# Two transformer blocks on one NeuronCore: one plain fp32 matmul in place of three rounded fp32 ones, and four weight slots filled in one order

## What is computed

```python
def first_block(x, c, ctx, ...):
    sh1, sc1, g1, sh2, sc2, g2 = adaln(c, w_ada)          # six vectors of 1024
    hc = modulate(rms_norm(ctx), ...)                     # 256 context tokens
    s_f, s_b = hgrn2_context_states(hc @ w_in ...)        # start states of the scans
    hx = modulate(rms_norm(x, norm_mix), sh1, sc1)
    mx = token_mix(hx)       # hx @ w_in (1024 x 4096), gated scans in two directions,
                             # a 3-tap convolution, then @ w_out (1024 x 1024)
    x = x + g1 * mx
    x = x + g2 * expert_choice_ffn(...)   # 16 experts, 64 tokens each, width 2048
    return rms_norm(x, norm_final)

def second_block(x, p, ...):
    z = rmsnorm(x, g_mix) @ w_in_2        # 1024 x 4376
    h = x + (ga * attention(z) @ w_o + gb * conv31(z) @ w_conv_out) @ w_out_2
    v = causal_dwconv(rmsnorm(h, g_ffn) @ w_up_2)         # 1024 x 5632
    h = h + (gelu(v_gate) * v_val) @ w_down_2             # 2816 x 1024
    h = h + sigmoid(rmsnorm(h, g_ple) @ w_ple_gate) * (p @ w_ple)
    return rmsnorm(h, g_final)
```

## Time and profile before

| | |
|---|---|
| Median of three runs | 2591.15 us |
| The profiled execution's own time | 2587.63 us |
| Its span, first to last instruction | 2585.7 us |
| Mean granted TensorE clock | 0.931 |
| TensorE busy with matmuls (PE) / weight loads (PEld) | 2221.8 us (86%) / 1390.3 us (54%) |
| VectorE / ScalarE / GpSimd busy | 900.8 / 564.9 / 368.1 us |
| Split of the weights: ScalarE L354, VectorE L360, GpSimd L367 | 163.0 / 211.6 / 235.8 us |
| Moved by DMA | 529.07 MB |

### The profile page before, as it was taken

One profiled execution on the slowest core, in us unless ns is written; L12 is line 12 of the kernel. 1 busy time (PEld: TensorE's weight loads), 2 busy tenths in 40 slices (PEclk: granted clock), 3 DMA queues, 4 the chain that ended last, 5 costly groups with the idle time before them and its releaser, 6 DMA issues.

```text
span 2585.7 us, 23858 instructions
## 1 busy us (share of the span) xinstructions
PE 2221.8 (86%) x10085; PEld 1390.3 (54%) x10085; DVE 900.8 (35%) x1266; ACT 564.9 (22%) x872; POOL 368.1 (14%) x261
## 2 busy tenths in 40 slices
PE   5999988778887878787878777899889989999987
PEld 3887766433232324232323222478557867887865
DVE  3435545400100101010101010477785537665443
ACT  3442303200000000000000000431545324333443
POOL 4111201000000000000000000130432413223530
PEclk8999989789899999998989898998889999999999
DMA  7121415379999999999999999134001223332220
GB/s 252 55 72 38 164 36 205 118 279 369 340 376 360 379 367 358 372 374 350 371 356 366 371 344 371 69 83 131 1 33 65 98 73 98 98 98 90 90 82 33
DMA packets 248017, 529.07 MB, mean 205 GB/s; under 512 B 13091, under 2 KB 41481, under 8 KB 247912
## 3 DMA queue, kind: packets, MB, share of 16 engines
q1 hardware_dynamic: 247336, 527.09, 56.4%
q0 software_dynamic: 576, 0.46, 0.1%
HBM read 525.43 MB, written 2.10 MB: 204 GB/s over the span
## 4 chain that ended last, share of the span: by engine, by line
PE 62%; DMA 19%; DVE 8%; ACT 5%; issue 4%; POOL 1%; SPq 0%; ACTq 0%; DVEq 0%
PE bank L849 12%; PE bank L511 10%; PE bank L512 10%; PE bank L513 10%; DMA f<-in_w_up_dram 9%; PE bank L889 8%; DMA f<-in_w_gate_dram 8%; PE bank L522 2%; PE bank L757 2%; DVE r L360 1%; DMA f<-in_w_down_dram 1%; PE bank L823 1%; PE bank L714 1%; PE bank L724 1%; PE bank L560 1%
## 5 line engine op out<-in xcount | busy, mean ns | idle before, releaser
L849 PE MATMUL bank<-f,high 128*64 128x512 f32 x2048 | 499.3, 644 | 124.3 <-DMA f<-in_w_gate_dram 65.6
L367 POOL TENSOR_TENSOR r<-f,r 128x1024 fp32r<-128x1024 f32 (+3 forms) x86 | 235.8, 2762 | 1819.0 <-ACT r L354 1818.9
L511 PE MATMUL bank<-r 128*128 128x512 f32 (+1 forms) x952 | 381.1, 400 | 39.3 <-DVE r L1984 12.9
L849 PEld LDWEIGHTS bank<-f,high 128*64 128x64 f32 x2048 | 173.1, 148 | 432.1 <-issue 422.2
L513 PE MATMUL bank<-r 128*128 128x512 f32 (+1 forms) x1016 | 401.4, 395 | 0.0
L512 PE MATMUL bank<-r 128*128 128x512 f32 (+1 forms) x952 | 377.1, 396 | 0.0
L889 PE MATMUL bank<-f,high 128*64 128x512 f32 x1024 | 259.6, 665 | 91.3 <-issue 80.5
L360 DVE TENSOR_TENSOR r<-f,r 128x1024 fp32r<-128x1024 f32 (+3 forms) x86 | 211.6, 2497 | 101.5 <-ACT r L354 101.5
L1928 DVE SCALAR_TENSOR_TENSOR f<-bank,low,f 128x512 f32<-128x512 f32 x64 | 48.1, 751 | 520.4 <-PE bank L837 516.8
L511 PEld LDWEIGHTS bank<-r 128*128 128x128 f32 (+1 forms) x952 | 181.3, 190 | 87.6 <-issue 33.8
L889 PEld LDWEIGHTS bank<-f,high 128*64 128x64 f32 x1024 | 90.7, 153 | 255.0 <-issue 255.0
(11 more groups left out here) (311 smaller groups left out, 2074.4 us busy)
## 6 DMA issues: line engine op xcount, KB each, us to landing
f<-in_w_down_dram SPq DMA_DIRECT2D x68, 2048.0 KB, 10.7
f<-in_w_gate_dram SPq DMA_DIRECT2D x64, 2048.0 KB, 12.6
f<-in_w_up_dram SPq DMA_DIRECT2D x64, 2048.0 KB, 12.5
f<-in_w_in_dram SPq DMA_DIRECT2D x15, 2048.0 KB, 7.8
f<-in_w_ada_dram SPq DMA_DIRECT2D x12, 2048.0 KB, 9.5
f<-in_w_up_dram SPq DMA_DIRECT2D x22, 1024.0 KB, 7.0
f<-in_w_out_dram SPq DMA_DIRECT2D x4, 2048.0 KB, 8.3
high<-in_x_dram SPq DMA_DIRECT2D x4, 1024.0 KB, 6.1
```

Of the source, the lines that this page charges most:

```text
L367: up(g.tensor_tensor(low_part(c)[:, z], whole(c)[:, z], high_part(c)[:, z].bitcast(F32), ALU.subtract), "lo_g", c, i)
L511: pe.matmul(o, wh, xh, start=first, stop=False)
L849: ins = pe.matmul(o[64 * e:64 * e + 64, :], xsT[p % 2][:, k, 64 * e:64 * e + 64], ws[e][:, k, :], start=k == 0, stop=k == 7)
```

## The change

Every product of `three` becomes one plain fp32 matmul of the undivided tiles. The split of weights and tokens goes, with its instructions on ScalarE, VectorE and GpSimd. All chunks of the kernel, the first two modulation slices and the experts' included, form one list; chunk c lies in slot c % 4, and a load waits for the last use of chunk c - 4. The normed tokens are written once (U1, U2) and kept; the second norm after attention goes. x is no longer loaded a second time: its raw transpose into XT is made at the start (32 more transposes there, 4 more copies on ScalarE and 4 on VectorE), and the 32 transposes and 8 copies before the output projection go. SBUF regions of the second block move.

```diff
-            def three(o, wh, wl, xh, xl, first, last):
-                pe.matmul(o, wh, xh, start=first, stop=False)
-                pe.matmul(o, wl, xh, start=False, stop=False)
-                return pe.matmul(o, wh, xl, start=False, stop=last)
...
+            def tiles(c, nk, n=512):
+                if c not in ready:
+                    ready.add(c)
+                    pe.wait_ge(s[f"w{c % 4}"], landed[c])
+                return whole(c)[:, 0:nk * n].rearrange("p (k n) -> p k n", k=nk)
...
-            def project(o, c, j, xh, xl, nk=8, m=128):
-                wh, wl = tiles(c, nk)
-                z = slice(128 * j, 128 * j + m)
+            def project(o, w, c0, x_, nk=8, m=128):
                 for k in range(nk):
-                    weights(c, k, nk)
-                    ins = three(o, wh[:, k, z], wl[:, k, z], xh[:, k, :], xl[:, k, :], k == 0, k == nk - 1)
+                    ins = pe.matmul(o, w[:, k, c0:c0 + m], x_[:, k, :], start=k == 0, stop=k == nk - 1)
                 return ins
...
         def whole(c):
-            return own(SLOT, slot_at[2 * pair[c]])
+            return own(SLOT, slot_at[c % 4])
...
+            load_chunk(0)
+            load_chunk(1)
+            for c in (2, 3):
                 for dst, src in cols(I["w_ada"][0], 512 * c, 512)(early[c]):
                     sp.dma_start(dst, src).then_inc(s[f"ada{c}"], 16)
...
+            load_chunk(VI)
+            for c in range(4, len(chunks)):
+                last_use = chunks[c - 4][1]
+                sp.wait_ge(s[last_use[0]], val(*last_use))
                 load_chunk(c)
...
+                pe.wait_ge(s[f"x{t // 2}"], 16)
+                for half in range(2):
+                    o = take(("xw", t, half), "v_pre" if half else "a_pre", "xw", t, half)
+                    up(turn_blocks(o, [xtok[:, t, 512 * half + 128 * j:512 * half + 128 * j + 128] for j in range(4)]),
+                       "pe_pre", "xw", t, half)
...
-            for t in range(4):
-                pe.wait_ge(s[f"x{t // 2}"], 32)
-                for half in range(2):
-                    o = take(("xr", t, half), "a_mix", "xr", t, half)
...
             def normed(gen, d, gain, r_):
-                if d > 1:
-                    name = "u2l_g" if d % 2 else "u2l_v"
-                    v.wait_ge(s[name], val(name, gen, d - 2))
-                f = FTS[gen][d % 2]
...
+                up(v.scalar_tensor_tensor(out=U2[:, d, :], in0=XT[:, d, :], scalar=gain[:, d:d + 1], in1=r_, op0=ALU.mult,
+                                          op1=ALU.mult), "u2", gen, d)
```

More of the change, by code:

```diff
@@ L76, in build_program @@
         cursor = [0]
-        rounded, full = {}, {}
+        full = {}
         def mem(n, at_=None):
@@ L133, in build_program @@
         stage = v3(mem(5 * 128, M + 11264), 5)
[L134 to L137, removed]
+        adatmp = [mem(512, M + 26624 + 512 * i) for i in range(2)]
+        U1 = v3(own(4096, M + 14336), 8)
         CF = v3(own(2048, M + 12288), 8)
@@ L342, in low_part @@
-        def low_part(c):
-            return memR(SLOT, slot_at[2 * pair[c]])[:, 0:chunks[c][1]]
-        def quarter(c, i):
-            step = chunks[c][1] // 4
-            return slice(step * i, step * i + step)
-        def a_divide(a, c, pieces=range(4)):
-            for i in pieces:
-                if i == 0:
-                    a.wait_ge(s[f"w{pair[c]}"], landed[c])
-                z = quarter(c, i)
-                up(a.activation(high_part(c)[:, z], whole(c)[:, z], ACT.Copy), "hi", c, i)
@@ new lines, in chunk, with ada_chunk @@
+        def chunk(parts, *last_use):
+            chunks.append((parts, last_use))
+            return len(chunks) - 1
+        def ada_chunk(c):
+            return chunk(cols(I["w_ada"][0], 512 * c, 512), "pe_ada", c)
+        ada_at = {c: ada_chunk(c) for c in range(2)}
+        ZF = chunk(cols(win, 512, 512), "pe_proj", "cgate", 0, 1)
+        VI = chunk(cols(win, 1536, 512), "pe_proj", "vctx", 1)
+        ZB = chunk(cols(win, 1024, 512), "pe_proj", "sigb", 3)
+        QC = chunk(cols(win, 0, 512), "pe_proj", "q", 3)
@@ new lines, in build_program @@
+        for p in range(8):
+            for fc in range(4):
+                for kind in range(2):
+                    for e in range(2):
+                        w = I["w_up" if kind else "w_gate"][0, 2 * p + e]
+                        moe_at[p, "up", kind, fc, e] = chunk(cols(w, 512 * fc, 512), "pe_up", p, kind, fc)
+            for kc in range(4):
+                for e in range(2):
+                    moe_at[p, "down", kc, e] = chunk(rows(I["w_down"][0, 2 * p + e], 512 * kc, 4), "pe_down", p, kc)
@@ L661, in conv_half @@
                 o = banks[bank_of["cv", which, j]]
-                wh, wl = tiles(c, 8)
-                z = slice(128 * j, 128 * j + 128)
+                w = tiles(c, 8)
                 for k in range(4 * part, 4 * part + 4):
-                    weights(c, k, 8)
-                    ins = three(o[:, :], wh[:, k, z], wl[:, k, z], UH[:, k, :], UL[:, k, :], k == 0, k == 7)
+                    ins = pe.matmul(o[:, :], w[:, k, 128 * j:128 * j + 128], U1[:, k, :], start=k == 0, stop=k == 7)
                 if part:
@@ L879, in tensor @@
                 for kc in range(4):
-                    n = 24 * p + 16 + 2 * kc
-                    ws = []
-                    for e in range(2):
-                        pe.wait_ge(s[f"m{(n + e) % 4}"], 16 * ((n + e) // 4 + 1))
-                        ws.append(v3(own(SLOT, slot_at[(n + e) % 4]), 4))
+                    ws = [tiles(moe_at[p, "down", kc, e], 4, D) for e in range(2)]
                     pe.wait_ge(s["hT"], val("hT", p, 3))
```

685 lines of the change are left out of this document (152 added, 533 removed).

## The result

The change makes the kernel slower: 2741.62 us (median of 4 runs, 2739.34 to 2744.05) against 2590.37 (4 runs, 2586.69 to 2592.34), a ratio of 1.0586 with a 95% interval of 1.0567 to 1.0604. The prediction was 2767 us with a range of 2738 to 2805: the side and the price of a product are right, the time is 25 us too long, and part of the relief came by another way than I had said. The profiled execution took 2744.05 us, its span is 2742.3.

A forecast was written before the change was run, and what follows sets the result against it. TensorE was taken to bound everything outside the experts, DMA the experts. The profiled 2587.6 us + 246 for dearer products - 70 for stalls gave 2764; with the median 3.5 us above the profiled run, 2767 us, range 2738 to 2805.

The forecast's parts named there:

- The price of a product: TensorE outside the experts: 0.858 us plain against 0.680 for three rounded matmuls, +246 us in all, bounds +235 to +287.
- Rival 2: Plain fp32 products cost 0.887 us each, as read from the experts: +40 us, 2807 us; chance 9%.
- rival 1: Passes of plain fp32 overlap, a product costs under 0.731 us and the kernel gets faster; chance 3%.
- rival 3: TensorE's clock falls under long fp32 work, a twentieth of it running low: +60 us, 2827 us; chance 3%.
- Rival 4: One order of slots lets the expert stage run at 379 GB/s, 1062 us, so 2725 us in all; chance 5%.
- Rival 5: Shortened chains are held by something else, so only -35 us of stalls go: 2802 us; chance 7%.
- The relief: TensorE stalls outside the experts that go with the split, plus small gaps among a product's three matmuls: -70 us.
- The start: -0.5: Before the first product: about 4 us of split wait go, 3.5 us of added transposes and copies stay: -0.5 us.
- Between the scans: Gap from forward scan's end through gates and convolution tiles: 39.8 us becomes about 33; with hidden product cost, -13 us.
- Output projection: After the last scan work: copies no longer behind a split, x's transposes gone; 9.6 us plus 2.9 overcharged, -12 us.
- The scores before the first scan: TensorE's 5.82 us wait behind VectorE's split and gates shrinks, a late copy remaining: -5 us.
- The waits at the merge, at the down projection and in attention: TensorE waits of 5.74, 3.19 and 3.23 us tied to splits or rounding: -8, -6 and -5 us.

The follow-up runs named there:

- Experiment 2: Changed kernel with three rounded matmuls of one constant tile per product, split still gone: 2504.1 us, ratio 0.9679 to the kernel before.
- experiment 5: Changed kernel with each fp32 product cut into two matmuls of 64 stationary columns, side by side: 2744.03 us against 2741.62.
- experiment 3: Changed kernel with loads outside the experts waiting for the chunk two before, not four: 2740.03 us against 2741.62.
- Experiments 1: Kernel before with splits and their waits kept, one plain fp32 matmul replacing the three rounded ones: 2792.34 us, ratio 1.0797.
- experiment 4: Changed kernel without its 32 extra transposes at the start: 2739.18 us; kernel before with 32 such transposes added: 2581.52 us, ratio 0.9978.

## Why the prediction was right, and where it was off

- **The price of a product: right.** Predicted 0.858 us, measured 0.859; the FFN's up stage (352 products) took 303.9 us where I had said 302. Experiment 2 against the changed kernel shows 243.6 us for the exchange alone, predicted 246; the medians give 237.5.
- **Rival 2 (0.887, as in the experts): wrong**, by the products' pace, by experiment 5 in the tiled form, and by the experts' own loads: 0.887 was a misreading of the earlier trace rows, and so was the upper bound of the price, 287 us, that rested on it; the 0.443 in rival 1 likewise is 0.429. Rival 1 (overlap, below 0.731) and rival 3 (the clock falls under long fp32 work) did not come: the clock in the FFN was 0.99 to 1.00.
- **Rival 4 (experts gain) and the four slots: nothing.** 1100 us as before, and experiment 3. Rival 5 (stalls stay) did not come either.
- **The relief: the term that was mis-sized.** Predicted 70, measured 88 in the profiles. The step that failed is "The start: -0.5"; it was -10.0. I had 4 us for the split and measured 7.7: I counted one split, and the chain had ScalarE's rounding, VectorE's share of the weights and the first tile's split in a row. And I charged 3.5 us for the transposes "at the low clock", while they kept the clock up and brought 2.3.
- **The other stalls, one by one.** Between the scans: 31.2 us remain where I had said 33, so -14.3 with the hidden products, predicted -13. Output projection: 25.7 us from the scans' end to its second part became 17.1, so -11.5, predicted -12. The scores before the first scan: 5.82 + 0.17 became 0.27 + 1.67, -4, predicted -5. The waits at the merge, at the down projection and in attention (5.74, 3.19 and 3.23) are gone, as predicted; of the norm chains one lost 5.25 us altogether, another only 1.4 (5.08 to 3.69). With the start these are most of what makes 131 us of idle time 74. The 6 us of small gaps between the three, which I called a guess, were some 10 (experiment 2).
- **Part of the relief is clock.** Outside the experts the clock rose from 0.93 to 0.96 ahead of them and from 0.96 to 0.98 behind; 0.03 of 490 us and 0.02 of 1000 us are about 35 us, an estimate that the rounding of the clock to 0.01 leaves open by some 10. With 57 us less idle time that makes 92 against the 88, so the two explain the relief within this error, and no finer split can be read from them.
- **What I had attributed wrongly.** I took all the relief for the removed split. Experiments 1 and 2 show that about 39 of the 88 us come with the plain product alone, some 30 of them because slower products hide splits without removing them. That does not change the forecast's sum, but it is another mechanism than the one I gave.
- **A term that I had not seen.** The second scan took 8 us longer than in other runs of the same code, because its modulation slices ran at the low clock (below). Without it the profiled execution would have been 8 us shorter, and the relief 96 instead of 88.

## What to carry to other kernels

Before pricing a leaner scheme, find the engine that sets the end and price only what the change does to it: here 835 us of work vanished from three other engines and bought at most 84 us, while 0.18 us more for each of 1384 products cost 244. To price the removal of side work, run both halves of the change alone: the value of a removed stall depends on how long the work beside it lasts. Read a price from start to start: the length of a merged group has the last record's overhang in it. And when a chain in front of a busy engine shortens, add up all the links that stand ahead of it in each queue, not only the one of the same name.

## What was not expected of the hardware

Transposes hold TensorE's clock. With 32 more of them in the kernel before, the granted clock from 22 to 37 us was 1.00 where it had been 0.92, 0.74 and 0.66, and the same 16 matmuls took 1.92 us in three of four slices instead of one; the first product came 0.9 us earlier in spite of the added work. The Trainium skill (TensorE: Matmul & The Clock Gate, Part 4: PE-mode transpose) says that the full clock does not engage for transposes, since they don't count as busy in the same way; the runs of experiment 4 disagree for these fp32 transposes, from both sides.

The clock in the scans differs from run to run of the same instructions. The second scan's steps with modulation slices, in 10 us windows: first the changed kernel, then the run with two slots, which has the same work there:

```profile
405.00:415.00 10.00, 10.00 (x57) 6.53 (x56) 2.41 (x9) 0.60 (x1) 0.00 (x0) 0.66 0.83 310
415.00:425.00 10.00, 10.00 (x57) 6.19 (x56) 2.42 (x9) 0.60 (x1) 0.00 (x0) 0.66 0.60 210
```

```profile
405.00:415.00 10.00, 10.00 (x88) 7.39 (x88) 4.22 (x14) 0.60 (x1) 0.00 (x0) 1.00 0.92 331
415.00:425.00 10.00, 10.00 (x84) 7.26 (x77) 3.53 (x13) 1.19 (x2) 0.00 (x0) 1.00 0.93 333
```

From the second scan's scores to the output projection it is 89.9 us in the one and 81.8 in the other, and 81.8 too in the changed kernel without the transposes. What tips a run to the one side or the other stays open.

An fp32 product of 128x512 takes the same 0.858 us as one matmul of 128 stationary columns and as two of 64 side by side.
